# One inference step of a hybrid decoder layer: row buffers stored from GpSimd's queue, and the samples' logits made on GpSimd

## The reference

```python
h = _rmsnorm(x, norm_g) * (1.0 + scale) + shift
z = einsum("nld,de->nle", h, w_in)            # width 3840, split into 14 parts
a = _pool_mix(...); b = dilated attention; c = _short_conv(...); d = window attention
x + gate * einsum("nle,ed->nld", concat(branch * silu(gate_path)), w_out)
```

```python
s = einsum("nthgd,ntjhd->nthgj", q, kg) * (1.0 / math.sqrt(dh))
s = s - slopes[:, :, None] * dists
```

## Time and profile before

| | us |
|---|---|
| median of 3 runs | 1443.58 (1442.41 to 1443.98) |
| the profiled execution's own time | 1442.13 |
| its span, first to last instruction | 1440.5 |
| TensorE busy | 1317.1 (91%) |
| VectorE busy | 720.6 (50%) |
| ScalarE busy | 465.4 (32%) |
| GpSimd busy | 217.8 (15%) |
| mean granted TensorE clock | 0.965 |

### The profile page before, as it was taken

One profiled execution on the slowest core, in us unless ns is written; L12 is line 12 of the kernel. 1 busy time (PEld: TensorE's weight loads), 2 busy tenths in 40 slices (PEclk: granted clock), 3 DMA queues, 4 the chain that ended last, 5 costly groups with the idle time before them and its releaser, 6 DMA issues.

```text
span 1440.5 us, 21453 instructions
## 1 busy us (share of the span) xinstructions
PE 1317.1 (91%) x7749; PEld 1143.1 (79%) x7749; DVE 720.6 (50%) x1859; ACT 465.4 (32%) x1213; POOL 217.8 (15%) x264
## 2 busy tenths in 40 slices
PE   5869999999999999988899995998989988999896
PEld 2359999999999999987899874776767647877774
DVE  3492122100335454222221474886989646888784
ACT  4440000121111011211211373676649631343431
POOL 0060000000121211000000033216203410111111
PEclk9989999999999999999999996999899998999999
DMA  8624121121343534377752996853924364555531
GB/s 295 219 88 147 44 87 69 62 87 44 117 174 134 176 103 138 99 196 186 185 151 64 305 256 194 270 170 87 291 82 129 124 222 126 161 178 165 166 125 45
DMA packets 137558, 214.62 MB, mean 149 GB/s; under 512 B 13731, under 2 KB 85060, under 8 KB 135277
## 3 DMA queue, kind: packets, MB, share of 16 engines
q1 hardware_dynamic: 124326, 168.51, 37.8%
q0 software_dynamic: 13152, 45.09, 9.4%
HBM read 136.34 MB, written 77.35 MB: 148 GB/s over the span
## 4 chain that ended last, share of the span: by engine, by line
PE 56%; issue 15%; DVE 10%; SPq 8%; DMA 4%; ACT 4%; POOL 2%; DVEq 0%; POOLq 0%; ACTq 0%
PE psum L1001 13%; PE psum L1002 13%; PE psum L1003 13%; SPq L726 3%; PE psum L1134 3%; PE psum L1118 2%; PE psum L1107 2%; PE psum L972 2%; DMA dil_v_p<-kv_nat 2%; DVE logits L1779 2%; ACT probs L1385 2%; PE psum L1108 2%; PE psum L1143 1%; POOL resid L948 1%; SPq L439 1%
## 5 line engine op out<-in xcount | busy, mean ns | idle before, releaser
L1001 PE MATMUL psum<-h_hi,w_hi 128*128 128x416 f32 (+1 forms) x1200 | 424.4, 354 | 29.8 <-DVE k_nat L1631 16.2
L1002 PE MATMUL psum<-h_lo,w_hi 128*128 128x416 f32 (+1 forms) x1200 | 421.8, 351 | 0.0
L1003 PE MATMUL psum<-h_hi,w_lo 128*128 128x416 f32 (+1 forms) x1200 | 420.1, 350 | 0.0
L1001 PEld LDWEIGHTS psum<-h_hi,w_hi 128*128 128x128 f32 x1200 | 227.3, 189 | 36.1 <-issue 32.9
L1002 PEld LDWEIGHTS psum<-h_lo,w_hi 128*128 128x128 f32 x1200 | 227.3, 189 | 1.5
L1003 PEld LDWEIGHTS psum<-h_hi,w_lo 128*128 128x128 f32 x1200 | 227.2, 189 | 1.4
L1385 ACT ACTIVATE probs<-logits,stats 128x256 f32<-128x256 f32 (+1 forms) x352 | 162.1, 462 | 129.4 <-DVE stats L1779 120.8
L1779 DVE CUSTOM_DVE_ANT_0 logits<-psum,bias_dil 128x256 f32<-128x256 f32 (+1 forms) x288 | 93.4, 361 | 69.7 <-PE psum L1108 57.2
L1001 PE MATMUL psum<-wo_hi,y_hi 128*128 128x512 f32 x288 | 116.9, 406 | 11.6 <-DVE y_lo L1848 11.5
L1003 PE MATMUL psum<-wo_hi,y_lo 128*128 128x512 f32 x288 | 114.0, 396 | 0.0
L1002 PE MATMUL psum<-wo_lo,y_hi 128*128 128x512 f32 x288 | 113.7, 395 | 0.0
(11 more groups left out here) (251 smaller groups left out, 1814.9 us busy)
## 6 DMA issues: line engine op xcount, KB each, us to landing
w_raw<-w_tiles POOLq DMA_DIRECT2D x30, 512.0 KB, 6.6
k_both<-k_dram SPq DMA_DIRECT2D x12, 1024.0 KB, 7.8
q_both<-q_dram SPq DMA_DIRECT2D x20, 512.0 KB, 6.8
mix_dram<-o_st POOLq DMA_DIRECT2D x36, 264.0 KB, 3.9
mix_in<-mix_dram SPq DMA_DIRECT2D x16, 594.0 KB, 3.9
gate_dram<-main SPq DMA_DIRECT2D x9, 1024.0 KB, 3.9
x_in<-x_prompt SPq DMA_DIRECT2D x16, 512.0 KB, 5.9
ada_w<-w_ada SPq DMA_DIRECT2D x4, 2048.0 KB, 10.1
```

The lines of the kernel that those rows point to most:

```text
L1001: pe.matmul(out, hi, mhi, start=start, stop=False)
L1002: pe.matmul(out, hi, mlo, start=False, stop=False)
L1003: return pe.matmul(out, lo, mhi, start=False, stop=stop)
```

## The change

It has three parts. First, `nat_store` moves from SP's queue to GpSimd's: it is called at the end of `load`, behind the weights' load and `chunk_load` of the same step, instead of at the head of SP's `store`. Second, all of the samples' logits move from DVE to GpSimd, which has no sum along a row here: `sums` adds halves, 64 to 32 and so on, in six additions, each waited for, since the next reads it. `row_logits`, `window_logits` and `new_logits` run in two steps each, in steps of GpSimd's loop that lie in phases without gathers: `ROW_STEPS` 49, 53, 57, 61, 65, 69, 73 and 113, `WINDOW_STEPS` 117 and 120, `OWN_STEPS` 123 and 124. Third, the wait for `dec_loaded` and the first two loads of `dec_k` come at step 47 instead of 31; each later `dec_k` is loaded behind the product of the row two before.

```diff
-        ROW_GROUPS, ROW_STEPS = (4, 5, 7, 8), (36, 38, 46, 50)
+        ROW_STEPS, WINDOW_STEPS, OWN_STEPS = (49, 53, 57, 61, 65, 69, 73, 113), (117, 120), (123, 124)
 # SP: store
-                for n, g in turns(ts - 1) if ts >= 12 else ():
-                    nat_store(n, g, ts - 1)
 # GpSimd: load
                 n = ts - CHUNK0
                 if 0 <= n < NCH:
                     chunk_load(n)
+                for n, g in turns(ts - 1) if ts >= 12 else ():
+                    nat_store(n, g, ts - 1)
 # GpSimd: mix
-                if i < 2 and y in ROW_GROUPS:
-                    x = ROW_GROUPS.index(y)
-                    if x == 0:
-                        pool.wait_ge(dec_loaded, 16 * DEC_LOADS)
...
+            def link(ins):
+                links[0] += 1
+                ins.then_inc(dec_link, 1)
+                pool.wait_ge(dec_link, links[0])
+            def sums(out, products):
+                v = products.rearrange("p (x e) -> p x e", e=64)
+                for w in (32, 16, 8, 4, 2):
+                    link(nc.gpsimd.tensor_tensor(v[:, :, 0:w], v[:, :, 0:w], v[:, :, w:2 * w], ALU.add))
+                link(nc.gpsimd.tensor_tensor(out.unsqueeze(2), v[:, :, 0:1], v[:, :, 1:2], ALU.add))
+            def row_logits(n, step):
+                prod = dec_prod[:].rearrange("p (c e) -> p c e", c=3)
+                if step == 0:
+                    pool.wait_ge(dec_k_loaded[n % 2], 48 * (n // 2 + 1))
+                    link(nc.gpsimd.tensor_tensor(prod, dec_k[n % 2][:], dec_q[:, n:n + 1, :].broadcast_to([P, 3, 384]), ALU.mult))
+                    if n + 2 < NS:
+                        row_load(n + 2)
+                else:
+                    sums(dec_red[:].rearrange("p c h -> p (c h)"), dec_prod[:])
+                    link(nc.gpsimd.tensor_scalar(dec_red[:], dec_red[:], 0.125, None, ALU.mult))
+                    nc.gpsimd.tensor_tensor(dec_s[:, :, 6 * n:6 * n + 6], dec_red[:],
+                                            consts[:, C_DB:C_DB + 18].rearrange("p (c h) -> p c h", c=3), ALU.add)
...
+            def decode(s):
+                if s == ROW_STEPS[0] - 2:
+                    pool.wait_ge(dec_loaded, 16 * DEC_LOADS)
+                    for n in range(2):
+                        row_load(n)
+                for x in range(2):
+                    if s - x in ROW_STEPS:
+                        row_logits(ROW_STEPS.index(s - x), x)
+                    if s - x in WINDOW_STEPS:
+                        window_logits(WINDOW_STEPS.index(s - x), x)
+                if s in OWN_STEPS:
+                    new_logits(OWN_STEPS.index(s))
...
             for s in range(UNITS + MIX_LAG):
                 if s < UNITS and units[s].d > 1:
                     gather(s, units[s])
+                decode(s)
                 if s >= MIX_LAG and (s - MIX_LAG) % 4 == 0:
                     mix((s - MIX_LAG) // 4)
 # DVE: decode and the loop
-                if s == 0:
-                    dve.wait_ge(dec_link, ROW_LINKS * NS)
-                    dve.sem_inc(dec_s_ready, 1)
-                    dve.wait_ge(lo_stored[1], 16 * lo_stores(NT + 1))
-                if 0 <= s < 2:
-                    window_logits(s)
-                if s == 2:
-                    new_logits()
...
-                if s < LAST and s % 64 in ROW_STEPS:
-                    row_logits(s // 64, ROW_STEPS.index(s % 64))
```

More of the change, by code:

```diff
@@ L673, in _ @@
                 sp.dma_start(gate_w[q][:], wv[:, 2 * q:2 * q + 2, 2 * D:3 * D]).then_inc(gate_loaded[q], 16)
[L675 to L689, removed]
             def first_pieces():
@@ L917, in mix @@
                 pool.dma_start(dst, o_st[g % 2][:]).then_inc(mix_stored[g % 2], 16)
-                if i < 2 and y in ROW_GROUPS:
-                    x = ROW_GROUPS.index(y)
-                    if x == 0:
-                        pool.wait_ge(dec_loaded, 16 * DEC_LOADS)
[L922 to L927, removed]
+            links = [0]
@@ new lines, in link @@
+            def link(ins):
+                links[0] += 1
+                ins.then_inc(dec_link, 1)
+                pool.wait_ge(dec_link, links[0])
+            heads = lambda ap, n: ap.rearrange("p (s h) -> p s h", h=n)
+            def sums(out, products):
[3 more added lines that the diff above has]
+                link(nc.gpsimd.tensor_tensor(out.unsqueeze(2), v[:, :, 0:1], v[:, :, 1:2], ALU.add))
@@ new lines, in row_load @@
+            def row_load(n):
+                for c in range(3):
+                    pool.dma_start(dec_k[n % 2][:, c, :], cache_rows(dil_kc, n, c)).then_inc(dec_k_loaded[n % 2], 16)
+            def row_logits(n, step):
[5 more added lines that the diff above has]
+                        row_load(n + 2)
+                else:
+                    sums(dec_red[:].rearrange("p c h -> p (c h)"), dec_prod[:])
+                    link(nc.gpsimd.tensor_scalar(dec_red[:], dec_red[:], 0.125, None, ALU.mult))
+                    nc.gpsimd.tensor_tensor(dec_s[:, :, 6 * n:6 * n + 6], dec_red[:],
+                                            consts[:, C_DB:C_DB + 18].rearrange("p (c h) -> p c h", c=3), ALU.add)
@@ new lines, in window_logits @@
+            def window_logits(half, step):
+                prod = dec_prod[:, 0:1024]
+                part = slice(16 * half, 16 * half + 16)
+                if step == 0:
+                    link(nc.gpsimd.tensor_tensor(
+                        prod.rearrange("p (y x e) -> p y x e", x=2, e=64),
+                        dec_sq[:, 1024 * half:1024 * half + 1024].rearrange("p (y x e) -> p y x e", x=2, e=64),
+                        dec_sk[:, 8 * half:8 * half + 8, :].unsqueeze(2).broadcast_to([P, 8, 2, 64]), ALU.mult))
+                    return
+                sums(dec_ss[:, part], prod)
+                v = heads(dec_ss[:, part], 4)
+                link(nc.gpsimd.tensor_scalar(dec_ss[:, part], dec_ss[:, part], 0.125, None, ALU.mult))
+                nc.gpsimd.tensor_tensor(v, v, consts[:, C_SB:C_SB + 4].unsqueeze(1).broadcast_to([P, NS // 2, 4]), ALU.add)
@@ new lines, in new_logits @@
+            def new_logits(x):
+                own, full, q, k, rows, n = ((dec_own, dec_s4, dec_qn[:], dec_kn[:], 24, NHD),
+                                            (dec_sown, dec_ss4, dec_sqn[:],
+                                             dec_skn[:].rearrange("s g x e -> s (g x e)"), NS, NHS))[x]
+                pr = dec_prod[0:rows, 0:64 * n]
+                link(nc.gpsimd.tensor_tensor(pr, q, k, ALU.mult))
+                sums(own[:], pr)
+                link(nc.gpsimd.tensor_scalar(own[:], own[:], 0.125, None, ALU.mult))
+                nc.gpsimd.tensor_tensor(heads(full[:], n), own[:].unsqueeze(1).broadcast_to([rows, NS, n]),
+                                        consts[0:rows, C_NEW:C_NEW + NS].unsqueeze(2).broadcast_to([rows, NS, n]),
+                                        ALU.add).then_inc(dec_s_ready, 1)
@@ L1656, in _ @@
             heads = lambda ap, n: ap.rearrange("p (s h) -> p s h", h=n)
[L1658 to L1681, removed]
```

28 lines of the change are left out of this document (13 added, 15 removed).

## The result

| | before | after |
|---|---|---|
| median of four runs, us | 1443.78 (1442.41 to 1444.37) | 1409.15 (1399.44 to 1412.32) |
| the profiled execution's own time | 1442.13 | 1399.44 |
| its span | 1440.5 | 1397.8 |
| GpSimd busy | 217.8 | 311.9 |
| VectorE busy | 720.6 | 699.9 |

The changed kernel is faster: 0.975 of before, 95% interval 0.9701 to 0.98. The profiled execution is the fastest of its four. The others took 8 to 13 us longer at a mean clock of 0.973 to 0.978, and the last experiments show where.

What follows compares the result with a forecast made beforehand. It priced only places where TensorE stands still, in projection and attention. From 1442.1 us: row buffers -20, dec_loaded -15, row logits off DVE -12, windows and new rows -8, GpSimd's lag +14.5, giving 1402; 8-in-10 range 1382 to 1430.

Steps and rivals of the forecast that it cites:

- Row buffers, k tiles, 22 less: Projection's k tiles: kv_nat stores no longer queue behind SP's k_dram issues, tiles go to 24.7 us, about 22 us less.
- v tiles, 2 given back: Projection's v tiles: stores come behind yac_ready and five loads on GpSimd, 1 us longer in each of two tiles.
- dec_loaded, 15 less: Attention, first gather phase: with dec_loaded waited for at unit 47, nothing is waited for, 15 us less.
- DVE's rows out of the gather phases, 3 and 3: Attention: 3 us less in each of two pairs' gather phases, with the phase ends 12 us less together.
- Windows and new rows, 8 less, with cover: Attention, four units of 18.9 us: 8 us less if GpSimd has dec_s_ready in time, with 5 us of cover.
- GpSimd's lag, 14.5 more: Units 47 to 79: a row costs GpSimd 10.7 us where four units take 7.25, 14.5 us more by unit 80.
- Row 7.8 (GpSimd keeps up): Rival for GpSimd's rows: 7.8 us each without fixed time, the 14.5 comes off, total 1387; chance 0.15.
- Transfers bind the k tiles at 179 GB/s: Rival for the k tiles: a tile takes 30.9 us, the 22 shrink to 4, total 1420; chance 0.13.
- GpSimd shut out at 16.5 us a row: Rival for units 48 to 79 and 113 to 124: GpSimd steps run as slowly as L866, total 1459; chance 0.07.

Runs made afterwards that it cites:

- Experiment 1: Kernel before with only nat_store moved to GpSimd's queue, the samples' logits left on DVE: 1424.95 us, 0.9879 of before.
- experiment 2: Changed kernel with nat_store put back on SP's queue, ahead of SP's stores: 1424.43 us, 0.9896 of before.
- Experiment 4: Changed kernel with the row buffers' stores ahead of chunk_load on GpSimd's queue instead of behind it: 1403.14 us, 0.9723 of before.
- Experiment 5: Kernel before with the dec_k loads and the dec_loaded wait begun at step 47 instead of 31, DVE's rows after them: 1427.53 us, 0.9903 of before.
- experiment 9: Kernel before with row buffers stored by GpSimd and keys fetched from step 47 on, all logits on DVE: 1408.45 us, 0.9763 of before.
- experiment 8: Changed kernel run again without edit: 1405.48 us, 0.9735 of before.
- experiment 6: Changed kernel with the halvings of the row sums left out, so output is not the reference's: 1394.56 us, 0.9676 of before.
- experiment 10: Changed kernel without edit, beside the kernel that keeps all logits on DVE: 1406.32 us, 0.9743 of before.
- experiments 3: Changed kernel with GpSimd's rows six units apart instead of four, two rows pushed into the next gather phase: 1405.59 us, 0.9761 of before.
- experiment 7: Changed kernel with row buffers ahead of chunk loads, GpSimd making product and first halving, DVE summing the rest: 1393.04 us, 0.9646 of before.

## Why the prediction was right

The forecast of 1402 us was 7 under the median and 2.6 over the profiled execution of the changed kernel; its sum was made from the profiled execution before. The mechanisms were the ones named, but that the total came so close is in part luck: in the table of stretches the terms are off by up to 3 us in both directions and cancel, and the profiled execution is the fastest of its four. Point by point:

- *Row buffers, k tiles, 22 less.* Right in its mechanism: 24.7 us a tile, the third copy 8.4 us after the first (some 9 forecast), no wait for k_nat. Experiment 1 shows it alone, experiment 2 its absence.
- *v tiles, 2 given back.* The place was right, the size was not: tiles 19 and 20 lose 2.0 and 4.1 us, 6.2 together, where before lost 1.4. The term was "1 us longer in each of two tiles"; it is 4.7 in the two. Experiment 4 takes all of it away by the order alone.
- *dec_loaded, 15 less, and DVE's rows out of the gather phases, 3 and 3.* Together 20.3 and 5.7 measured, 18 and 3 predicted. Experiment 5 shows nearly all of it from the two lists of its diff, with DVE still at work. The rows' share was put too low: the sum gave a gather phase without them 28 us, but the earlier trace rows has one, steps 79 to 95, that takes 994.01 - 968.33 = 25.7.
- *Windows and new rows, 8 less, with cover.* The stretch of steps 131 to 135 fell by 7.5 us, and TensorE had no wait for dec_s_ready. Beside experiment 9, which leaves them on DVE, 127 to 143 is 9.7 us shorter.
- *GpSimd's lag, 14.5 more.* The row was 10.40 us (10.7 predicted). The window half was 6.8 us, 7.8 with its mix store, where 7.8 had been worked out without one. GpSimd was to have gathered for unit 80 at 77.6 us after the mix store of step 47; TensorE started the unit at 78.1, and at 77.7 in experiment 8. So the term was right in cause and size. Only the way was other than I had put it: of the gather 0.7 us was left to wait for in the first profile and 2.3 in experiment 8, and TensorE had stood before that, where ACT waited for the mix stores and GpSimd held DVE's tables, a hold that the sum doesn't have. Measured at 47 to 95: 98.9, against 91.2 with rows on DVE and 86.9 with short rows. The total of experiment 6 puts it at 10.9; its first four units still wait for keys.
- *Rivals.* Row 7.8 (GpSimd keeps up): measured 10.4, out. Transfers bind the k tiles at 179 GB/s: they move 229, out. GpSimd shut out at 16.5 us a row: out; the product beside DVE's logits took 2.64 to 2.89 us, and from 870 to 944 us those logits took 422 and 480 ns by kind, as in the same units before (421 and 479). The Trainium skill, "SBUF — State Buffer", section "Who interferes with whom", says a DVE instruction with at most one SBUF input, outside its two-port modes, doesn't contend with GpSimd; for the logits, which read their scores from PSUM, the rows agree. The rival asked only whether GpSimd would be slowed. The tables show the other way round: DVE held for 2.75 us by GpSimd's product. Whether they run in such a mode no run here shows.

The 0.2% that the prediction gave as what a measurement can tell from no change was too fine: the intervals here are 0.3 to 0.5% either way.

What the sum could not say is how little the move itself is worth. I priced it as one block with the later fetch and the sparing of the gather phases. Apart, the row buffers and the two changed step lists give 0.9763, the whole 0.9743. The windows' 9.7 us are paid for by the lag's 7.7, and sometimes by the clock after it. The reason is in two rows: the product takes 1355 ns in the median on DVE in the kernel before and 2712 on GpSimd, 2.00 times as long, and behind it come eight dependent steps, six additions, scale and bias, where DVE had a sum of 1353 ns and one small operation. The Trainium skill, "GPSIMD Engine Reference", section 4.1, advises VectorE for elementwise work and gives GpSimd as about twice as slow for operations with two inputs; the measurement is in line with it.

The 7 us between forecast and median go, as far as the traces show, with the clock. At unit 80 the executions of experiments 8 and 10 took 102.9 and 103.1 us for 47 to 95, the first profile 98.9. Late, experiment 4 has a clock of 0.50 from 1076 to 1092 with TensorE busy throughout, where the first profile shows 1.00. One window of the first profile, against the last line of experiment 8's:

```profile
1084.00:1092.00 8.00, 7.69 (x61) 5.70 (x62) 4.68 (x28) 5.39 (x25) 4.89 (x8) 1.00 0.18 55
```

Matmuls fall from 61 to 44 in eight us. Experiment 4 lost 8.5 us there (93.1 from step 143 to the last mix store against 84.6), experiment 10 nothing (84.8). The first place goes with the lag: around unit 80 the clock falls in all five profiles in which GpSimd has made seven full rows by then (the first, experiments 2, 4, 8 and 10), and stays at 1.00 in experiments 3, 6, 7 and 9, where it has less to do. The late one is in eight of the twelve profiles, experiments 1 and 9 with all logits on DVE among them, so it isn't the move's. Why one execution has it and another doesn't stays open: no run changed what TensorE does ahead of it.

## What to carry to other kernels

Before work is moved to a slower engine, try first to move only its time: here a list of step numbers and the queue of one store gave all but 2 of 37 us (experiments 9 and 10), and the move of the arithmetic, with nine dependent steps a row, paid for itself and no more. Price a moved chain by the period it must keep (10.4 us against 7.25) and split it where the period breaks, as experiment 7 does, with a buffer for each side if there is room. A store put on another queue inherits that queue's waits: its place in the step, ahead of or behind the waiting loads, was worth 6 us of tile time.

## What was not expected of the hardware

- A fixed cost on GpSimd is small: an addition of 18 elements takes 0.22 to 0.23 us, one with a scalar 0.28, and from the end of one step to the start of the next that waits for it are some 0.1 us (891.07 + 0.22 to 891.39). The estimate had 0.3 and 0.1.
- TensorE's granted clock can be low while TensorE is busy: 0.50, the lower of its two levels (1.2 GHz of 2.4), for the 16 us from 1076 in experiment 4, busy in all of them, and 0.58 and 0.57 in the mean of two windows of 6 us around unit 80 in experiment 8, busy for 4.86 and 6.00. There the 6 us before show it busy for 3.80.
- GpSimd can hold a DVE instruction that has one tile to read: two of the bias tables took 2.75 and 2.31 us beside a product and an addition on GpSimd, 0.35 elsewhere. The rows stand in the section on the result.
- The gathers have a maximum of 1.67 us in the changed kernel too, where DVE no longer makes row products. DVE's and GpSimd's timelines show the other instruction with two SBUF inputs, the split of the output weights:

```profile
1062.26 1.68 DVE L1761 TENSOR_TENSOR wo_lo<-wo_raw,wo_hi 128x1024 fp32r<-128x1024 f32 x1
```
```profile
1061.65 2.79 POOL L997 CAST q_ring<-q_both 128x256 fp32r<-128x256 f32 x3
```

Three gathers in a row took 2.79 us, where three of 0.65 are 1.95, and the split 1.68, where it takes 1.22 in the median. Both engines lose where they meet, as the gather at 891.83 in the earlier trace rows lost beside DVE's product, 1.60 us instead of 0.64.
